# A fourth split slot in the down stage of two feed-forward layers, in place of two sum buffers

## The chip, the cores and the metric

The kernel runs on one core of one Trainium2 chip. The metric is the device time of one execution in microseconds (us), read as the median of several executions.

## The reference

The reference is one transformer block on 256 tokens of width 2048: a first feed-forward layer, a mixer, a second feed-forward layer, each with a residual and a layer norm. The change lies in the down projection of both feed-forward layers, the last product of

```python
def swiglu(x, w_gate, w_up, w_down):
    return (jax.nn.silu(x @ w_gate) * (x @ w_up)) @ w_down
```

Here `x` is [256, 2048], the two first weights are [2048, 5632] and `w_down` is [5632, 2048], all in float32.

## The kernel before

**Precision and units.** Every float32 operand is cut into a high part (rounded by ScalarE) and a low part (the rest, made by VectorE), and each product takes three matmuls: high by high, high by low, low by high. The weights are streamed. A unit is two 128-row tiles of 512 columns (`UNIT_KT` = 2, 512 KB). For one unit SyncE loads it into one of 8 raw slots (`load_unit` L386, and L847 to L857 for the down stage), ScalarE writes its high part into one of 3 split slots (`whi`, `split_hi` L436 to L444), VectorE its low part (`wlo`, `split_lo` L446 to L452), and TensorE multiplies it with two halves of 128 tokens (`token_mm` L454 to L466): 2 tiles x 2 halves x 3 = 12 matmuls of 512 columns. TensorE counts finished units in the semaphore `unit_used`; ScalarE waits for it before it writes a split slot again (L443, L1053). VectorE counts low parts in `lo_done`; TensorE waits for that before a unit, and SyncE before it loads a raw slot again.

**The down stage** of layer f runs twice over w_down, for output columns 0 to 1023 (pair 0) and 1024 to 2047 (pair 1); in a pair, c = 0 and 1 are the two chunks of 512 columns. The 5632 rows are 22 units. Most are multiplied as above ("plain"). But 2 x 3 units in pair 0 and 2 x 4 in pair 1 are taken in quads (`QUADS` L205): units a = 4+q and b = 8+q with both chunks are a 2 x 2 block product of 128 tokens by 512 columns, done with 7 products instead of 8 in Strassen's manner. Such a product ("form", P1 to P7) is 6 matmuls, half of a plain unit. P1, P2 and P3 use raw weights; P5, P7, P6 and P4 use differences of weight blocks that VectorE makes first (`add`, L1146 to L1167): P5 = (a,1)-(a,0), P7 = (b,1)-(a,1), P6 = (b,1)-P5's sum, P4 = (b,0)-P6's sum. P7's is written over the raw slot of (a,1), the three others into the three buffers of `sumB` (L261). `MADE` and `made` count them in the semaphore `formed`. The token side needs sums too, S1 to S4, made once per layer from `hT` in the first items of pair 0 (`sums` L1195, `sum_hi` L1056, `sum_lo` L1188; the same `sumB` buffers hold them on the way); P3, P5, P6 and P7 wait for them (L975).

**The order of work** is written out by hand in the class `Pair` (L49 to L103). `items` is the order in which all three engines take units and forms, `raws` the order of the loads. A pair begins with plain units (10 in pair 0, 2 in pair 1); then each quad comes as a group of 7 forms mixed with 4 plain units (3 in the last group), in the order U P1 P5 U P7 P3 U P6 P2 U P4; then come the plain units that are left (the tail, from index `tail`). Pair 0 has 53 items, pair 1 has 56. The split slot of an item is that of `ring_place` (L106): item number modulo 3, but with one step back in the middle of a phase, at item 27 of pair 0 and item 29 of pair 1, which take the slot of the item two places earlier, and not three. A raw slot is loaded again once the low part of the last item that reads it is made (`released_by` L90); SyncE issues the loads in order, so one that waits holds back all behind it. The last 6 items of pair 1 have split places of their own (`edge`) and are multiplied in half passes (`down_exit` L511).

**VectorE's order** (`down_pair` L1284): for each item the sum of a form a little ahead (for P5 before the low part of the item ahead of P1's end, for P7 and P6 behind P5 and P7, for P4 one item ahead of P6), then the low part (`form_lo` L1169 or `split_lo`), then a step of the token sums (pair 0, items 2 to 9), then in the tail a step of the fold: accumulators and the four product banks of `tp` are added into `resid` (`down_add` L1222, `fold` L1252, `down_stats` L1236). Two adds of pair 0 are done behind items 2 and 3 of pair 1 (L1307).

## Time and profile before

| what | value |
|---|---|
| median of 3 executions | 1941.09 us (1940.5 to 1942.88) |
| the profiled execution | 1941.81 us, its span 1939.8 us |
| TensorE busy | 1909.5 us, 98% of the span |
| VectorE busy | 1253.9 us, 65% |
| ScalarE busy | 894.1 us, 46% |
| granted TensorE clock, mean of the span | 0.998 |
| down stage of layer 1, layer 2 | about 494 to 703 us, about 1688 to 1928 us of the span |

Matmul records overlap: one of 512 columns shows 0.39 us, but the next starts 0.227 us after it. So a gap on TensorE is best read from the starts of two matmuls. `idle before` leaves out a part of it, because the modelled end of a matmul lies behind the next one's usual start. In the profile PE is TensorE, PEld its weight loads, DVE VectorE, ACT ScalarE, POOL GpSimd, SP SyncE.

### The profile page before, as it was taken

What the parts mean: (1) busy time and instruction counts of PE and PEld (TensorE: products, weight loads), DVE (VectorE), ACT (ScalarE), POOL (GpSimd) and SP (SyncE); (2) the same over time, 40 slices, a digit from 0 to 9 for tenths busy, and PEclk for the clock granted to TensorE, in tenths of its full rate; (3) what the DMA queues carried; (4) which work ended last, traced back from release to release, by engine and by line L of the source; (5) the groups of instructions that cost most, each with busy time, mean ns of one, the idle gap of its engine ahead of it and who ended that gap; (6) DMA issues with size and microseconds to landing.
All of it is one profiled execution on the core that took longest, in us unless ns stands there. A gap on an engine that the chain in (4) does not pass through costs nothing.

```text
span 1939.8 us, 27987 instructions
## 1 busy us (share of the span) xinstructions
PE 1909.5 (98%) x10490; PEld 1617.4 (83%) x10490; DVE 1253.9 (65%) x1411; ACT 894.1 (46%) x996; POOL 66.9 (3%) x93
## 2 busy tenths in 40 slices
PE   9999999999999999999999999999999999999997
PEld 8888888888778778999999888888888888877776
DVE  5555554555887887676766958555554555587887
ACT  5444443444454553545644544444444444455452
POOL 0000000000000001300131000000000000000000
PEclk9999999999999999999999999999999999999999
DMA  8666666667565665655442067566666666545654
GB/s 304 193 187 189 189 185 189 178 193 235 157 211 182 214 219 171 212 181 161 127 133 89 23 225 243 171 186 182 186 190 197 192 187 188 189 163 184 206 190 168
DMA packets 185365, 357.37 MB, mean 184 GB/s; under 512 B 11328, under 2 KB 23616, under 8 KB 184272
## 3 DMA queue, kind: packets, MB, share of 16 engines
q1 hardware_dynamic: 183600, 347.43, 57.4%
q0 software_dynamic: 1696, 8.99, 1.4%
q8 instruction: 47, 0.77, 0.2%
q14 instruction: 22, 0.18, 0.0%
HBM read 354.28 MB, written 2.10 MB: 184 GB/s over the span
## 4 chain that ended last, share of the span: by engine, by line
PE 91%; DVE 5%; issue 1%; DMA 1%; ACT 1%; POOL 0%; POOLq 0%; SPq 0%; DVEq 0%; ACTq 0%
PE acc L463 23%; PE acc L465 23%; PE acc L464 23%; PE acc L486 3%; PE acc L488 3%; PE acc L490 3%; PE tp L985 1%; PE tp L987 1%; PE tp L986 1%; DVE wlo L451 1%; PE tp L917 1%; PE acc L985 1%; PE acc L987 1%; PE acc L986 1%; ACT whi L444 1%
## 5 line engine op out<-in xcount | busy, mean ns | idle before, releaser
L451 DVE TENSOR_TENSOR wlo<-raw,whi 128x1024 fp32r<-128x1024 f32 (+2 forms) x579 | 692.5, 1202 | 602.8 <-ACT whi L444 600.7
L444 ACT ACTIVATE whi<-raw 128x1024 fp32r<-128x1024 f32 (+2 forms) x579 | 596.6, 1037 | 815.3 <-PE acc L465 726.9
L463 PE MATMUL acc<-whi,xT 128*128 128x512 f32 (+2 forms) x1644 | 631.0, 384 | 0.8 <-ACT zab L1612 0.4
L465 PE MATMUL acc<-whi,xT 128*128 128x512 f32 (+2 forms) x1644 | 625.7, 381 | 0.0
L464 PE MATMUL acc<-wlo,xT 128*128 128x512 f32 (+2 forms) x1644 | 625.2, 380 | 0.0
L463 PEld LDWEIGHTS acc<-whi,xT 128*128 128x128 f32 x1644 | 308.7, 188 | 64.7 <-issue 1.8
L465 PEld LDWEIGHTS acc<-whi,xT 128*128 128x128 f32 x1644 | 308.7, 188 | 59.5
L464 PEld LDWEIGHTS acc<-wlo,xT 128*128 128x128 f32 x1644 | 308.9, 188 | 55.8
L463 PE MATMUL acc<-whi,hT 128*128 128x512 f32 x432 | 170.8, 395 | 6.7 <-DVE wlo L451 6.7
L464 PE MATMUL acc<-wlo,hT 128*128 128x512 f32 x432 | 168.4, 390 | 0.0
L465 PE MATMUL acc<-whi,hT 128*128 128x512 f32 x432 | 168.4, 390 | 0.0
L486 PE MATMUL acc<-xT,whi 128*128 128x256 f32 x384 | 108.7, 283 | 0.0
L488 PE MATMUL acc<-xT,whi 128*128 128x256 f32 x384 | 108.7, 283 | 0.0
L490 PE MATMUL acc<-xT,wlo 128*128 128x256 f32 x384 | 108.7, 283 | 0.0
L463 PEld LDWEIGHTS acc<-whi,hT 128*128 128x128 f32 x432 | 81.1, 188 | 32.8 <-DVE wlo L451 16.4
L465 PEld LDWEIGHTS acc<-whi,hT 128*128 128x128 f32 x432 | 81.1, 188 | 17.4
L464 PEld LDWEIGHTS acc<-wlo,hT 128*128 128x128 f32 x432 | 81.2, 188 | 15.4
L1054 ACT ACTIVATE whi<-raw 128x1024 fp32r<-128x1024 f32 x56 | 59.4, 1061 | 39.3 <-PE acc L465 25.1
L1173 DVE TENSOR_TENSOR wlo<-raw,whi 128x1024 fp32r<-128x1024 f32 x56 | 67.4, 1221 | 11.6 <-ACT whi L1054 10.2
L490 PEld LDWEIGHTS acc<-xT,wlo 128*128 128x128 f32 x384 | 73.7, 192 | 0.0
L488 PEld LDWEIGHTS acc<-xT,whi 128*128 128x128 f32 x384 | 73.7, 192 | 0.0
L486 PEld LDWEIGHTS acc<-xT,whi 128*128 128x128 f32 x384 | 73.7, 192 | 0.0
(345 smaller groups left out, 1854.6 us busy)
## 6 DMA issues: line engine op xcount, KB each, us to landing
raw<-in_ffn_w_down_dram SPq DMA_DIRECT2D x176, 512.0 KB, 4.7
raw<-in_ffn_w_up_dram SPq DMA_DIRECT2D x175, 512.0 KB, 3.7
raw<-in_ffn_w_gate_dram SPq DMA_DIRECT2D x174, 512.0 KB, 3.8
raw<-in_w_in_dram SPq DMA_DIRECT2D x48, 512.0 KB, 3.9
raw<-in_w_out_dram SPq DMA_DIRECT2D x32, 512.0 KB, 6.4
raw<-in_w_in_dram SPq DMA_DIRECT2D x32, 260.0 KB, 2.8
raw<-in_w_in_dram SPq DMA_DIRECT2D x16, 456.0 KB, 5.2
raw<-in_w_q_idx_dram SPq DMA_DIRECT2D x8, 512.0 KB, 3.8
```

The source lines that it names most:

```text
L444: act.activation(hi[:, s, :, 0:w], raw[:, r, :, 0:w], ACT.Copy).then_inc(hi_done, 1)
L451: dve.tensor_tensor(lo[:, s, :, 0:w], raw[:, r, :, 0:w], hi[:, s, :, 0:w].bitcast(F32), ALU.subtract).then_inc(lo_done, 1)
L463: pe.matmul(o, hi, w_hi[:, s, k, 0:width], start=first and k == 0, stop=False)
L464: pe.matmul(o, hi, w_lo[:, s, k, 0:width], start=False, stop=False)
L465: ins = pe.matmul(o, lo, w_hi[:, s, k, 0:width], start=False, stop=last and k == UNIT_KT - 1)
L486: pe.matmul(o, whi[:, s, k, cols], hi, start=first and k == 0 and c == 0, stop=False, skip_group_check=True)
L488: pe.matmul(o, whi[:, s, k, cols], lo, start=False, stop=False, skip_group_check=True)
L490: ins = pe.matmul(o, wlo[:, s, k, cols], hi, start=False, stop=end, skip_group_check=True)
L985: pe.matmul(o, x_hi, w_hi[:, s, k], start=i == touches[0] and k == 0, stop=False)
L986: pe.matmul(o, x_hi, w_lo[:, s, k], start=False, stop=False)
L1054: act.activation(w_hi[:, s], form_raw(p, i), ACT.Copy).then_inc(hi_done, 1)
L1173: dve.tensor_tensor(w_lo[:, s], form_raw(p, i), w_hi[:, s].bitcast(F32), ALU.subtract)\
```

## The change

The group order becomes U P1 P3 P5 U P7 P6 U P2 P4 U, and the loads of a group U (a,0) (b,1) (a,1) U U (b,0) U. Pair 0 begins with 13 plain units, and its sums of tokens are spread over items 2 to 14. P6's sum is written over the raw slot of (a,0), P5's and P4's share one buffer `form_sum`, and the 8 KB per partition that two sum buffers took become a fourth split slot, used from item 16 of pair 0 on (before that the token sums lie there). `split_slots` hands out the split slots first in, first out, through both pairs, so an item of the groups and tails takes the slot of the item four places earlier; the step back in the middle is gone. VectorE makes each form's sum behind the low part of the item two places ahead. The raw slots of (a,0) and (b,0) are held until the low part of the item ahead of P4 (that is P2), (b,1) until that of the item ahead of P6. The fold takes P7's and P5's banks one by one: 8 counted steps in place of 7. The diff, cut:

```diff
@@ -63,13 +63,13 @@
             q = quads.index((a, b))
-            self.raws += [(a, 0), (a, 1), some[0], (b, 1), some[1], (b, 0), *some[2:]]
-            forms = [("P1", "P5"), ("P7", "P3"), ("P6", "P2"), ("P4",)]
+            self.raws += [some[0], (a, 0), (b, 1), (a, 1), *some[1:3], (b, 0), *some[3:]]
+            forms = [("P1", "P3", "P5"), ("P7", "P6"), ("P2", "P4"), ()]
...
                 self.items += [(form, q, 0) for form in forms[k]]
-        self.tail = len(self.items)
+        self.tail = 1 + max(i for i, item in enumerate(self.items) if item[0] == "P4")
@@ -85,12 +85,22 @@
         a, b = self.quads[x]
-        return self.raws.index({"P1": (a, 0), "P7": (a, 1), "P2": (b, 0), "P3": (b, 1)}[what])
+        return self.raws.index({"P1": (a, 0), "P6": (a, 0), "P7": (a, 1), "P2": (b, 0), "P3": (b, 1)}[what])
+    def item(self, form, q):
+        return self.items.index((form, q, 0))
...
-        return max(i for i, (what, _, _) in enumerate(self.items)
-                   if what not in ("P4", "P5", "P6") and self.raw_of(i) == r)
+        last = max(i for i, (what, _, _) in enumerate(self.items)
+                   if what not in ("P4", "P5") and self.raw_of(i) == r)
+        for q, (a, b) in enumerate(self.quads):
+            if self.raws[r] in ((a, 0), (b, 0)):
+                return max(last, self.item("P4", q) - 1)
+            if self.raws[r] == (b, 1):
+                return max(last, self.item("P6", q) - 1)
+        return last
@@ -101,6 +111,22 @@
+def split_slots(pairs, one_more_from, kept_apart):
...
+    free, places = list(range(SPLIT_SLOTS)), [{}, {}]
+    user = {}
+    for pair, plan in enumerate(pairs):
+        for i in range(len(plan.items) - (kept_apart if pair else 0)):
+            if (pair, i) == (0, one_more_from):
+                free.insert(0, SPLIT_SLOTS)
+            s = free.pop(0)
+            free.append(s)
+            places[pair][i] = s, user.get(s)
+            user[s] = pair, i
+    return places, user
@@ -205,8 +231,10 @@
     ENDS = [*range(4), *range(12, DOWN_U)]
-    PAIRS = [Pair(QUADS[:3], sorted(ENDS + [7, 11]), sorted(ENDS + [7, 11]), 10, (4, 4, 4)),
-             Pair(QUADS, ENDS, ENDS, 2, (4, 4, 4, 3))]
+    PAIRS = [Pair(QUADS[:3], sorted(ENDS + [7, 11]), sorted(ENDS + [7, 11]), 13, (4, 4, 4)),
+             Pair(QUADS, ENDS, ENDS, 2, (4, 4, 4, 4))]
+    FOURTH_FROM = 16
+    SPLITS, LAST_USER = split_slots(PAIRS, FOURTH_FROM, EDGES)
@@ -259,6 +287,9 @@
         sumB = mz("sumB", 88, [P, 3, UNIT_KT, BANK])
+        form_sum = mz("form_sum", 88, [P, UNIT_KT, BANK])
+        fourth_hi = mz("fourth_hi", 92, [P, 1, UNIT_KT, BANK], F32R)
+        fourth_lo = mz("fourth_lo", 96, [P, 1, UNIT_KT, BANK], F32R)
@@ -401,6 +432,17 @@
                 return edge_hi, edge_lo, slot, st.index(p, 0, edge_free(slot))
+            if plan_of(p) is not None:
+                f, pair = (0, 1)[p in DOWN[1]], (0, 1)[p in (F1DB, F2DB)]
+                s, before = SPLITS[pair][u] if u < n else (u - n, LAST_USER[u - n])
+                if before is not None:
+                    free = st.index(DOWN[f][before[0]], 0, before[1] + 1)
+                elif s < SPLIT_SLOTS:
+                    last = [v for v in range(2 * KU) if ring_place(v, 2 * KU, SPLIT_SLOTS) == s][-1]
+                    free = st.index(GU[f], GATE_CHUNKS - 1, last + 1)
+                else:
+                    free = None
+                return (whi, wlo, s, free) if s < SPLIT_SLOTS else (fourth_hi, fourth_lo, 0, free)
@@ -858,7 +900,7 @@
         SUM_ORDER = [0, 2, 1, 3]
-        FOLDS = 7
+        FOLDS = 8
@@ -869,7 +911,7 @@
-        SUM_STEPS = ["A21", "A22", "S1", "S1 low", "A11", "S3", "S2", "A12", "S4", "S3 low", "S2 low", "S4 low"]
+        SUM_STEPS = ["A21", "A22", "S1", "A11", "S1 low", "S3", "S2", "A12", "S4", "S3 low", "S2 low", "S4 low"]
@@ -896,9 +938,8 @@
-            name = plan_of(p).items[i][0]
-            if name in ("P5", "P6", "P4"):
-                return sumB[:, ("P5", "P6", "P4").index(name)]
+            if plan_of(p).items[i][0] in ("P5", "P4"):
+                return form_sum[:]
@@ -1050,7 +1091,10 @@
                     act.wait_ge(raw_loaded[v % RAW_SLOTS], st.loaded(p, 0, v))
-                act.wait_ge(unit_used, free)
+                if free is None:
+                    act.wait_ge(sem("formed"), summed(f, "S4 low"))
+                else:
+                    act.wait_ge(unit_used, free)
@@ -1069,18 +1113,19 @@
                     if p == DOWN[f][0]:
-                        if i == 4:
-                            sum_hi(0, 2)
...
                             hT_act(act, f, GATE_CHUNKS)
-                        if i == 8:
+                        if i == 7:
+                            sum_hi(0, 2)
+                        if i == 11:
                             sum_hi(1, 1)
+                        if i == 12:
                             sum_hi(2, 0)
-                        if i == 9:
+                        if i == 13:
...
@@ -1145,26 +1190,32 @@
-                first = p == DOWN[f][0] and q == 0
-                a, b = plan_of(p).quads[q]
+                pair, plan = DOWN[f].index(p), plan_of(p)
+                a, b = plan.quads[q]
+                corner = raw_ready(dve, p, a, 0)
                 if name == "P5":
-                    upper, left = raw_ready(dve, p, a, 1), raw_ready(dve, p, a, 0)
-                    if first:
-                        dve.wait_ge(sem("formed"), summed(f, "S4 low"))
-                    elif q == 0:
-                        dve.wait_ge(sem("formed"), folded(f, 0, FOLDS))
-                    dve.tensor_tensor(sumB[:, 0], upper, left, ALU.subtract).then_inc(sem("formed"), 1)
+                    upper = raw_ready(dve, p, a, 1)
+                    if q > 0:
+                        dve.wait_ge(lo_done, st.index(p, 0, plan.item("P4", q - 1) + 1))
+                        dve.wait_ge(hi_done, st.index(p, 0, plan.item("P4", q - 1) + 1))
+                    else:
+                        dve.wait_ge(sem("formed"), folded(f, 0, FOLDS) if pair else summed(f, "S4 low"))
+                    dve.tensor_tensor(form_sum[:], upper, corner, ALU.subtract).then_inc(sem("formed"), 1)
...
                     block, right = raw_ready(dve, p, b, 1), raw_ready(dve, p, a, 1)
+                    dve.wait_ge(sem("formed"), made(f, p, "P5", q))
...
                 if name == "P6":
+                    block = raw_ready(dve, p, b, 1)
+                    dve.wait_ge(lo_done, st.index(p, 0, plan.item("P1", q) + 1))
+                    dve.wait_ge(hi_done, st.index(p, 0, plan.item("P1", q) + 1))
                     dve.wait_ge(sem("formed"), made(f, p, "P5", q))
-                    dve.tensor_tensor(sumB[:, 1], raw_ready(dve, p, b, 1), sumB[:, 0], ALU.subtract)\
-                       .then_inc(sem("formed"), 1)
+                    dve.tensor_tensor(corner, block, form_sum[:], ALU.subtract).then_inc(sem("formed"), 1)
...
                     left = raw_ready(dve, p, b, 0)
+                    dve.wait_ge(lo_done, st.index(p, 0, plan.item("P5", q) + 1))
                     dve.wait_ge(sem("formed"), made(f, p, "P6", q))
-                    dve.tensor_tensor(sumB[:, 2], left, sumB[:, 1], ALU.subtract).then_inc(sem("formed"), 1)
+                    dve.tensor_tensor(form_sum[:], left, corner, ALU.subtract).then_inc(sem("formed"), 1)
@@ -1198,25 +1249,30 @@
                     sum_of(2, *block(B_KT, 1))
+                if i == 4:
...
                     sum_made(0, 2, 1, 2, ALU.add)
-                if i == 5:
-                    sum_lo(0, 2)
...
                     hT_dve(dve, f, GATE_CHUNKS)
+                if i == 7:
                     sum_of(0, *block(A_KT, 0))
-                if i == 7:
+                if i == 8:
+                    sum_lo(0, 2)
+                if i == 9:
...
                     sum_made(1, 1, 0, 1, ALU.subtract)
+                if i == 10:
                     sum_made(2, 0, 2, 0, ALU.subtract)
-                if i == 8:
+                if i == 11:
...
                     sum_of(2, *block(B_KT, 0))
+                if i == 12:
...
                     sum_lo(1, 1)
-                if i == 9:
+                if i == 13:
                     sum_lo(2, 0)
+                if i == 14:
@@ -1251,23 +1307,24 @@
-                last, u2 = sumB[:, 0, 0], sumB[:, 0, 1]
+                one, two = form_sum[:, 0], form_sum[:, 1]
...
                     dve.wait_ge(sem("sum_act"), sum_act(f, 4 + pair))
-                    fold_resid(pair, 0, 0, last)
-                    dve.tensor_tensor(u2, p_bank("P6"), last, ALU.add).then_inc(sem("formed"), 1)
+                    fold_resid(pair, 0, 0, one)
+                    dve.tensor_tensor(two, p_bank("P6"), one, ALU.add).then_inc(sem("formed"), 1)
...
                     dve.wait_ge(sem("formed"), folded(f, pair, 2))
-                    dve.tensor_tensor(sumB[:, 1], tp[:, 2:4], u2.unsqueeze(1).to_broadcast([P, 2, BANK]), ALU.add)\
-                       .then_inc(sem("formed"), 1)
+                    dve.tensor_tensor(one, p_bank("P7"), two, ALU.add).then_inc(sem("formed"), 1)
+                    dve.wait_ge(sem("formed"), folded(f, pair, 3))
+                    fold_resid(pair, 0, 1, one)
...
@@ -1286,22 +1343,15 @@
                 for i in range(LEAD if pair == 0 else 0, len(plan.items)):
-                    what, q, _ = plan.items[i]
-                    after = plan.items[i + 1] if i + 1 < len(plan.items) else ("", 0, 0)
-                    if after[0] == "P1":
-                        add(p, "P5", after[1])
-                    if what == "P5":
-                        add(p, "P7", q)
-                    if what == "P7":
-                        add(p, "P6", q)
-                    if after[0] == "P6":
-                        add(p, "P4", after[1])
-                    if what == "unit":
+                    if plan.items[i][0] == "unit":
...
                         sums(i)
+                    soon, of, _ = plan.items[min(i + 2, len(plan.items) - 1)]
+                    if soon in MADE:
+                        add(p, soon, of)
...
                     if pair == 1 and i in (2, 3):
```

## Rows read from the trace of the kernel before

**Rows 1.** The page's chain that ended last, shares of the span.

```profile
PE 91%; DVE 5%; issue 1%; DMA 1%; ACT 1%; POOL 0%; POOLq 0%; SPq 0%; DVEq 0%; ACTq 0%
```

**Rows 2.** Waits of TensorE, 494 to 722 us, then 1690 to 1940: total, times, longest.

```profile
PE acc L463 <- DVE wlo L451: 3.4, 3, 1.7
PE acc L985 <- DVE wlo L1173: 1.2, 1, 1.2
PE tp L985 <- DVE wlo L1173: 0.2, 1, 0.2
...
PE tp L985 <- DVE wlo L1173: 1.1, 1, 1.1
```

**Rows 3.** Timeline of TensorE at stalls: start, duration, instruction, idle before and releaser.

```profile
522.80 0.39 PE L465 MATMUL acc<-whi,hT 128*128 128x512 f32 x1
524.90 0.50 PE L463 MATMUL acc<-whi,hT 128*128 128x512 f32 x1 [1.71 <-DVE wlo L451]
525.24 0.39 PE L464 MATMUL acc<-wlo,hT 128*128 128x512 f32 x1
...
535.74 0.39 PE L987 MATMUL acc<-whi,sumA 128*128 128x512 f32 x1
536.07 0.50 PE L463 MATMUL acc<-whi,hT 128*128 128x512 f32 x1
...
556.54 0.39 PE L987 MATMUL acc<-whi,sumA 128*128 128x512 f32 x1
558.04 0.50 PE L463 MATMUL acc<-whi,hT 128*128 128x512 f32 x1 [1.11 <-DVE wlo L451]
...
1916.54 0.50 PE L463 MATMUL acc<-edge,hT 128*128 128x512 f32 x1 [0.82 <-DVE edge L451]
```

**Rows 4.** Timeline of ScalarE: plain units, then a form's high part, then item 27.

```profile
495.16 1.06 ACT L444 ACTIVATE whi<-raw 128x1024 fp32r<-128x1024 f32 x1 [1.72 <-PE acc L465]
497.88 1.06 ACT L444 ACTIVATE whi<-raw 128x1024 fp32r<-128x1024 f32 x1 [1.66 <-PE acc L465]
...
523.74 1.06 ACT L1054 ACTIVATE whi<-sumB 128x1024 fp32r<-128x1024 f32 x1 [2.11 <-DVE sumB L1156]
...
555.66 1.06 ACT L444 ACTIVATE whi<-raw 128x1024 fp32r<-128x1024 f32 x1 [3.13 <-PE tp L987]
```

**Rows 5.** Timeline of VectorE: end of the head, item 27, and a fold of pair 0.

```profile
519.99 2.35 DVE L1192 TENSOR_TENSOR sumA<-sumB,sumA 128x1024 fp32r<-128x1024 f32 x2
522.48 1.23 DVE L1156 TENSOR_TENSOR sumB<-raw 128x1024 f32<-128x1024 f32 x1
523.62 1.22 DVE L451 TENSOR_TENSOR wlo<-raw,whi 128x1024 fp32r<-128x1024 f32 x1
...
556.76 1.23 DVE L451 TENSOR_TENSOR wlo<-raw,whi 128x1024 fp32r<-128x1024 f32 x1 [1.14 <-ACT whi L444]
...
597.03 0.68 DVE L1258 TENSOR_TENSOR sumB<-tp,sumB 128x512 f32<-128x512 f32 x1
...
599.15 1.22 DVE L1261 TENSOR_TENSOR sumB<-tp,sumB 128x1024 f32<-128x1024 f32 x1
```

**Rows 6.** Three loads issued close together (L857): issue times, then us to landing; three windows.

```profile
L857 SPq DMA_DIRECT2D raw<-in_ffn_w_down_dram x3: 368/368/468, 1725.9 to 1727.0; - x3
...
DMA to landing us min/median/max: 3.9/4.9/5.5
...
L857 SPq DMA_DIRECT2D raw<-in_ffn_w_down_dram x3: 368/368/468, 532.6 to 533.8; - x3
...
DMA to landing us min/median/max: 4.0/5.7/7.8
...
L857 SPq DMA_DIRECT2D raw<-in_ffn_w_down_dram x3: 367/468/469, 1803.4 to 1804.3; - x3
...
DMA to landing us min/median/max: 5.1/7.4/8.8
```

**Rows 7.** Timeline of ScalarE at the start of pair 1 in layer 2.

```profile
1811.27 1.06 ACT L444 ACTIVATE whi<-raw 128x1024 fp32r<-128x1024 f32 x1 [3.71 <-DMA raw<-in_ffn_w_down_dram]
```

More of the change, by code:

```diff
@@ L1082, in ffn_act @@
                         act.wait_ge(unit_used, st.index(p, 0, plan.tail))
-                        act.activation(sumB[:, 0, 0], p_bank("P1"), ACT.Copy).then_inc(sem("sum_act"), 1)
+                        act.activation(form_sum[:, 0], p_bank("P1"), ACT.Copy).then_inc(sem("sum_act"), 1)
         def resid_add(dve, p, c, scale, in_phase, t):
@@ L1238, in down_stats @@
                 dve.wait_ge((acc0_free, acc1_free)[c][t], (n0, n1)[c][DOWN[f][pair]] + 1)
-                dve.wait_ge(sem("formed"), folded(f, pair, 5))
+                dve.wait_ge(sem("formed"), folded(f, pair, 4))
                 col = (2 * pair + c) * BANK
@@ L1252, in fold @@
             def fold(pair, step):
-                last, u2 = sumB[:, 0, 0], sumB[:, 0, 1]
+                one, two = form_sum[:, 0], form_sum[:, 1]
                 if step == 0:
                     dve.wait_ge(sem("sum_act"), sum_act(f, 4 + pair))
-                    fold_resid(pair, 0, 0, last)
-                    dve.tensor_tensor(u2, p_bank("P6"), last, ALU.add).then_inc(sem("formed"), 1)
+                    fold_resid(pair, 0, 0, one)
+                    dve.tensor_tensor(two, p_bank("P6"), one, ALU.add).then_inc(sem("formed"), 1)
                 if step == 1:
                     dve.wait_ge(sem("formed"), folded(f, pair, 2))
-                    dve.tensor_tensor(sumB[:, 1], tp[:, 2:4], u2.unsqueeze(1).to_broadcast([P, 2, BANK]), ALU.add)\
-                       .then_inc(sem("formed"), 1)
+                    dve.tensor_tensor(one, p_bank("P7"), two, ALU.add).then_inc(sem("formed"), 1)
+                    dve.wait_ge(sem("formed"), folded(f, pair, 3))
+                    fold_resid(pair, 0, 1, one)
                 if step == 2:
-                    dve.wait_ge(sem("formed"), folded(f, pair, 3))
-                    fold_resid(pair, 1, 0, sumB[:, 1, 0])
-                    fold_resid(pair, 0, 1, sumB[:, 1, 1])
+                    dve.tensor_tensor(two, p_bank("P5"), two, ALU.add).then_inc(sem("formed"), 1)
+                    dve.wait_ge(sem("formed"), folded(f, pair, 5))
+                    fold_resid(pair, 1, 0, two)
                 if step == 3:
-                    dve.tensor_tensor(last, p_bank("P5"), sumB[:, 1, 1], ALU.add).then_inc(sem("formed"), 1)
-                    dve.wait_ge(sem("formed"), folded(f, pair, 6))
-                    fold_resid(pair, 1, 1, last)
+                    dve.tensor_tensor(one, p_bank("P5"), one, ALU.add).then_inc(sem("formed"), 1)
+                    dve.wait_ge(sem("formed"), folded(f, pair, 7))
+                    fold_resid(pair, 1, 1, one)
             def pair_end(pair, i):
```

## The prediction

> **What bounds the kernel now.** The chain of waits comes first: 91% of it is TensorE [rows 1], so only what TensorE waits for can be won, and any idle time of the other engines is free. The waits of TensorE come next, and only in the two stretches of the down stage, which the change touches: 4.8 us in 5 waits in layer 1. In layer 2 the first two rows come again with the same numbers, the third is 1.1 instead of 0.2, and an edge item adds 0.8: 6.5 us in 6 waits. All are waits for a low part of VectorE [rows 2, 3]. The timeline says what a wait costs in full, read from the starts. The usual distance of two matmuls is 0.227 us. At 522.80 the next start is 2.10 later and the one after it 0.34 later: 1.87 + 0.11 lost, against 1.71 shown as idle [rows 3]. So each wait costs 0.27 more than its row. Besides, some units arrive just in time (535.74 to 536.07 is 0.10 too long, and so is the next distance), about 0.2 each, 4 or 5 times a layer, 0.9 in all. Lost and removable: layer 1 4.8 + 5 x 0.27 + 0.9 = 7.1 us, layer 2 6.5 + 6 x 0.27 + 0.9 = 9.0, together 16.1. That is the ceiling of the gain. The number of matmuls does not change.
>
> **Why it waits.** Four distances carry the rest. A plain unit takes TensorE 2.72 us (the high parts start at 495.16 and 497.88), a form half of that, 1.36; a group of 4 units and 7 forms 20.4. From the start of a high part to the start of its low part are 1.10 (555.66 to 556.76), from there to TensorE's start 1.28 (556.76 to 558.04), and VectorE starts an operation of 1024 elements every 1.14 when nothing holds it (522.48 to 523.62), 1.35 when it reads what the one before wrote (the second of the pair at 519.99 starts 1.14 later, the next at 522.48) [rows 3 to 5]. A high part starts some 0.2 after TensorE has left the item whose slot it takes. A form's own high part starts 1.26 behind the start of its sum (522.48 to 523.74) [rows 4, 5]. With three slots an item is thus ready 0.2 + 1.10 + 1.28 = 2.58 after the start of the item two before it, which leaves 0.14 where two forms lie between, and less than nothing where VectorE is busy with a sum, or at the step back in the middle, where the slot is that of the item two earlier.
>
> **The change, part by part.**
>
> 1. The end of the head. Two low parts of token sums and P5's sum stand ahead of the low part of item 10 [rows 5], and cost 1.98. They are spread now. I follow VectorE with t = 0 at TensorE's start of item 12, TensorE at 0, 2.72, 5.44 (P1), 6.80 (P3), 8.16 (P5), 9.52 (unit 17). VectorE starts: low 12 at -4.14 (slot-bound), S4, S3 low, low 13 at -0.72, S2 low, low P1 at 1.56, S4 low 2.70, P5's sum 4.05 (the 1.35), low P3 5.19 (ready 6.47, 0.3 early), low P5 6.42 (its high part waits for the sum), P7's sum 7.56, low 17 at 8.70, ready at 9.98: 0.46 late. With the restart 0.1: 0.56 stays. S1 to S4 are done by 3.9, before P3 needs them. ScalarE's work per item, at most two operations of 1.06, fits into 2.72.
>
> 2. The step back in the middle goes. In pair 0 it costs 1.37 (556.54 to 558.04, less 0.227, and 0.1) [rows 3]; item 29 of pair 1 is its twin, 1.44 with 0.83 behind it. Gain 3.6 a layer.
>
> 3. Four slots in the groups. An item may be ready 2.58 after the start of the item three before it. The tightest place is now the unit behind P1 P3 P5. With TensorE's U at 0: low P5 at 1.3 (slot free at 0.2), P7's sum 2.44, low U 4.02, ready 5.3 and wanted at 6.8. Every later item of the group is at least 1.5 early. VectorE has 15 operations a group, 15 x 1.14 = 17.1 of 20.4, the same number as before. So nothing stalls, as long as the weights are there.
>
> 4. The loads. This is the price. (a,0) is now held until P2's low part is made, and SyncE issues in order, so six of a group's eight loads go out together when P2's low part is done, and P5's sum of the next group needs (a,1), the third of them. From the landing of (a,1) to the end of P2's low part VectorE has 11 operations: 10 x 1.14 + 1.22 + 0.3 for two high parts that wait for sums + 0.1 = 13.0. A round is then 13.0 + L, L from the first issue to the third landing, against TensorE's 20.4. It binds when L is over 7.4. Three loads issued together are in the trace: twelve times within the groups, L from 6.6 (1725.9 to 1727.0 + 5.5) to 9.0 (532.6 to 533.8 + 7.8), median 7.5, mean 7.5. Once, with more queued ahead, it is 9.7 [rows 6]. Those third loads were issued 1.1 us behind the first, in the change it will be 0.8, which helps little where the transfers queue. In pair 0 the first group ends with its low P2 done at 16.84 in the count of part 1, so unit U of the next group is ready at 16.84 + L + 6.07, and wanted at 30.38: late by L - 7.46. The twelve values give 0.37 as the mean of this where positive. Twice per layer, 0.1 for a restart each: 0.94. In pair 1 the first group starts with all its weights there and low P2 done at 12.1 after its U, which leaves 1.5 us of slack before the same sum comes out late; over three rounds at the median nothing is lost.
>
> A page of the Trainium skill has this cheaper: DMA: Bandwidth & Descriptors, section on the anatomy of one DMA, gives about 2.0 us fixed and bytes / 436e3 per us. By it three loads of 524,288 bytes would take 5.6 us, an estimate, and the 0.94 a layer would be nothing; the sum below would be 1.9 us lower. No burst here was that quick, so the rows decide.
>
> 5. The start of pair 1. In layer 2 ScalarE waits 3.71 us for a load there [rows 7], VectorE's adds of pair 0 pile up behind it, and P5 comes 1.28 late (0.39 in layer 1). Now the first unit of the group is third in the loads, and the extra slot lets VectorE do the tail about one item earlier. VectorE: low of item 2 at -1.4 against TensorE's start of pair 1, its add at 0.2 (it waits for pair 0's last unit), low P1 1.4, P5's sum 2.55, add and statistics, low P3 4.9, low P5 6.7 (wanted at 10.9 - 1.28). The gain is all of it, 0.46 and 1.36. Behind the waiting add stands only low P1, whose slot is freed by the same event.
>
> 6. The fold. One operation of 1024 (1.22) becomes two of 512 (0.68) [rows 5], and one dependent pair more waits 0.2: 0.3 us of VectorE per pair, in items with 2.72 us of room. In pair 0 free: P1 of pair 1 needs the last fold only 11 us later. At the end of layer 2 VectorE must hand over six items at half distance; there a wait of 0.82 is seen [rows 3]. The fourth slot lets it be up to 2.7 earlier; I count the low part of item 53 ready about 1 us early, and the 1.08 gone. If that lead were not there, 1.08 + 0.3 would stay.
>
> **Sum.** Left per layer: 0.56 + 0.94 + 0.3 for items just in time = 1.8. Gain (7.1 - 1.8) + (9.0 - 1.8) = 12.5 us. The profiled execution (1941.81, span 1939.8) would come to 1929.3; it lies 0.7 over the median, and against the median I predict 1941.09 - 12.5 = 1928.6.
>
> **Rivals.**
>
> A. No load binds (L stays under 7.2). For it: five of the twelve bursts; the page cited above would have it so. Left per layer 0.56 + 0.2: gain 14.6, 1926.5.
>
> B. Bursts of six are slower than bursts of three or four, L about 8.5. For it: 9.7 where loads were queued ahead; against: the median 7.5. Pair 0 loses 1.04 + 1.1, pair 1 3 x 1.1 - 1.5 = 1.8, with restarts 4.4 a layer, with 0.56 + 0.3: 5.3. Gain 16.1 - 10.6 = 5.5: 1935.6.
>
> C. Slower: VectorE stands idle each round before P5's sum, waiting for the third load, and the loop of loads and sums takes the place of the slots as what bounds the groups. The point where it decides: each us of L over 7.4 costs 2 in pair 0 and up to 3 in pair 1. Loss before is 16.1, so break-even is at 8 a layer: 0.9 + 2 (L - 7.4) + 3 (L - 7.4) - 1.5 = 8, L = 9.1. At L = 10 it is 12.4 a layer, 24.8 in all: 8.7 slower, 1949.8. For it: 9.0 and 9.7 were seen; against: ten of twelve are at 8.2 or less.
>
> D. The stalls move but don't go: the head's dense stretch (S3 low to P7's sum, ten VectorE operations while TensorE does six items) starts later than I have it, because there are still three slots. Each 0.3 of delay counts in full, and all of it also delays the first burst. If it costs 2 us per layer more and the edge wait stays: gain 7, 1934.
>
> **How the numbers follow.** About 0.2% (3.9 us) is what a measurement of this kernel can tell from no change. Forecast 0.45, A 0.20, B 0.14, C 0.06, D 0.07; 0.08 for L near 9, where the two kernels come out within 0.2%. Faster by over 0.2%: 0.45 + 0.20 + 0.14 + 0.07 = 0.86; within 0.08; slower 0.06. The likeliest is 1928.6. The range reaches over A (below it only the 16.1, 1925.0) and B with some room: 1925.0 to 1936.5, which leaves out C and the cases near no change.
>
> **What would show it.** Right: TensorE's waits in the two stretches fall from 11 to about 6, all under 1 us; none at item 27 of pair 0 or 29 of pair 1, none at the edge. One of about 0.5 at the unit behind the first P5. ScalarE's waits for TensorE in the groups move to the item three before. VectorE idles before P5's sum of the second and later groups, with a load as releaser, for about 0 to 2 us; six loads of L857 stand together, the third landing 7 to 8 us after the first issue. Wrong: waits of TensorE at the same unit of every group, growing from group to group, would be B or C; waits in items 14 to 20 of pair 0 over 1 us would be D.

## The result, and the profile after

The changed kernel takes 1924.74 us (median of 4, 1923.87 to 1925.47) against 1941.88 us of the kernel before beside it (median of 4, 1940.5 to 1942.88): ratio 0.9912, 95% interval 0.9895 to 0.9929. That is 17.1 us, where 12.5 were forecast, and 0.26 us below the range. The direction and most of the steps hold; the size does not.

The page after, engines and chain:

```profile
PE 1903.5 (99%) x10490; PEld 1621.3 (84%) x10490; DVE 1256.1 (65%) x1415; ACT 893.1 (46%) x996; POOL 66.9 (3%) x93
...
PE 90%; DVE 5%; DMA 2%; issue 1%; ACT 1%; POOL 0%; POOLq 0%; DVEq 0%; ACTq 0%
```

The span fell by 16.8 us, 1939.8 to 1923.0, at the same granted clock of 0.998. The number of matmuls is the same. On the chain DMA has 2% where it had 1% [rows 1]. Three loads of down weights make most of it (start on the chain, us on it):

```profile
696.26 15.35 DMA raw<-in_ffn_w_down_dram
...
1730.71 7.32 DMA raw<-in_ffn_w_down_dram
...
1751.81 7.23 DMA raw<-in_ffn_w_down_dram
```

The last two are (a,1), the third load of two bursts of part 4 in layer 2. The first is one of the last loads of layer 1's down stage; the forecast has no term for it.

TensorE's waits after, in 494 to 722 us and then in 1680 to 1923 (total, times, longest), which answer to [rows 2]:

```profile
PE acc L505 <- DVE wlo L493: 0.4, 1, 0.4
...
PE acc L505 <- DVE wlo L493: 0.7, 2, 0.4
PE acc L505 <- DVE fourth_lo L493: 0.3, 1, 0.3
```

Of eleven waits four are left, none over 0.41. The timeline of TensorE shows two of them, at the unit behind the first P5 of layer 1 and at the unit behind the second P5 of layer 2:

```profile
537.71 0.39 PE L1028 MATMUL tp<-fourth_hi,sumA 128*128 128x512 f32 x1
538.50 0.47 PE L505 MATMUL acc<-whi,hT 128*128 128x512 f32 x1 [0.41 <-DVE wlo L493]
538.81 0.40 PE L506 MATMUL acc<-wlo,hT 128*128 128x512 f32 x1
...
1743.31 0.39 PE L1028 MATMUL tp<-whi,sumA 128*128 128x512 f32 x1
1744.02 0.51 PE L505 MATMUL acc<-fourth_hi,hT 128*128 128x512 f32 x1 [0.32 <-DVE fourth_lo L493]
```

The first unit starts 0.56 too late and its second matmul another 0.08; the other one 0.48 and 0.11. From the first matmul on hT to the start of the next stage, layer 1's down stage takes 233.4 us (494.85 to 728.23) instead of 242.8 (494.90 to 737.74); layer 2's, from its first to its last matmul, 232.5 (1679.40 to 1911.85) instead of 240.5 (1688.20 to 1928.68). The work between the two was 0.7 us longer in this execution, which makes up the 16.8. Of the 17.5 us by which the two stages are shorter, about 16.0 are waits read from the starts: 16.1 + 3.5 before (the 3.5 between 721 and 738 us, which the forecast had left out), 2.4 + 1.3 after. The other 1.5 are in distances of 0.23 to 0.25 us in the items behind a wait.

That stretch, TensorE's waits from 722 to 765 us of the kernel before:

```profile
PE tp L574 <- DVE resid L739: 1.9, 1, 1.9
PE acc L463 <- DVE edge L451: 0.8, 1, 0.8
...
```

and from 714 to 757 us of the changed one:

```profile
PE tp L616 <- DVE resid L781: 0.8, 1, 0.8
...
```

The edge item waited in layer 1 exactly as in layer 2, and behind it TensorE waited 1.9 us for the first normalised columns before their transposes. After the change the first is gone and the second is 0.8.

VectorE's timeline after: the first group of pair 0 in layer 1 (S4 low, P5's sum, the unit's low part), P5's sum and P2's low part of the next groups, then P5's sum of two groups of layer 2.

```profile
531.15 1.22 DVE L1243 TENSOR_TENSOR sumA<-sumB,sumA 128x1024 fp32r<-128x1024 f32 x1
532.50 1.23 DVE L1203 TENSOR_TENSOR form_sum<-raw 128x1024 f32<-128x1024 f32 x1
...
537.13 1.22 DVE L493 TENSOR_TENSOR wlo<-raw,whi 128x1024 fp32r<-128x1024 f32 x1
...
544.03 1.22 DVE L1224 TENSOR_TENSOR wlo<-raw,whi 128x1024 fp32r<-128x1024 f32 x1
...
552.64 1.23 DVE L1203 TENSOR_TENSOR form_sum<-raw 128x1024 f32<-128x1024 f32 x1 [0.48 <-DMA raw<-in_ffn_w_down_dram]
...
564.17 1.22 DVE L1224 TENSOR_TENSOR fourth_lo<-raw,fourth_hi 128x1024 fp32r<-128x1024 f32 x1
...
572.74 1.23 DVE L1203 TENSOR_TENSOR form_sum<-raw 128x1024 f32<-128x1024 f32 x1 [0.48 <-DMA raw<-in_ffn_w_down_dram]
...
1738.11 1.23 DVE L1203 TENSOR_TENSOR form_sum<-raw 128x1024 f32<-128x1024 f32 x1 [1.80 <-DMA raw<-in_ffn_w_down_dram]
...
1759.12 1.23 DVE L1203 TENSOR_TENSOR form_sum<-raw 128x1024 f32<-128x1024 f32 x1 [2.03 <-DMA raw<-in_ffn_w_down_dram]
```

P5's sum stands 1.35 behind S4 low, and the unit's low part 4.63 behind P5's sum (4.65 was worked out). In every later group VectorE waits for a load before P5's sum, as forecast. The round is 20.1 us in layer 1 (552.64 to 572.74), just under TensorE's 20.4, and 21.0 in pair 0 of layer 2. From P5's sum to the end of P2's low part is 12.75 (552.64 to 564.17 + 1.22); with about 0.1 from the landing to the sum it is 12.9, close to the 13.0 of part 4.

The loads, three of a burst in layer 1 and in layer 2 (the line that was L857 is L899):

```profile
L899 SPq DMA_DIRECT2D raw<-in_ffn_w_down_dram x3: 368/467/469, 545.3 to 546.2; - x3
...
DMA to landing us min/median/max: 4.5/5.4/6.4
...
L899 SPq DMA_DIRECT2D raw<-in_ffn_w_down_dram x3: 368/467/469, 1729.8 to 1730.7; - x3
...
DMA to landing us min/median/max: 4.2/6.2/7.3
```

The third lands 7.3 us after the first issue in layer 1, 8.2 in layer 2. The second burst of pair 0 gives 7.2 in layer 1 and again 8.2 in layer 2.

### The profile page after: what moved, and what is told of

Same layout as the page of the kernel before. It is cut to its first block, busy times and chain, and to the rows that moved or that the text cites. A ratio compares the mean times of both kernels' runs of the same rounds, so it can differ in the third digit from the quotient of the medians.

```text
span 1923.0 us, 28047 instructions
## 1 busy us (share of the span) xinstructions
PE 1903.5 (99%) x10490; PEld 1621.3 (84%) x10490; DVE 1256.1 (65%) x1415; ACT 893.1 (46%) x996; POOL 66.9 (3%) x93
## 4 chain that ended last, share of the span: by engine, by line
PE 90%; DVE 5%; DMA 2%; issue 1%; ACT 1%; POOL 0%; POOLq 0%; DVEq 0%; ACTq 0%
PE acc L505 24%; PE acc L507 24%; PE acc L506 24%; PE acc L528 3%; PE acc L532 3%; PE acc L530 3%; DMA raw<-in_ffn_w_down_dram 2%; PE tp L1026 1%; PE tp L1028 1%; PE tp L1027 1%; PE tp L958 1%; DVE wlo L493 1%; PE acc L1026 1%; PE acc L1028 1%; PE acc L1027 1%
## 5 line engine op out<-in xcount | busy, mean ns | idle before, releaser
L493 DVE TENSOR_TENSOR wlo<-raw,whi 128x1024 fp32r<-128x1024 f32 (+2 forms) x559 | 668.0, 1201 | 576.4 <-ACT whi L486 574.8
L486 ACT ACTIVATE whi<-raw 128x1024 fp32r<-128x1024 f32 (+2 forms) x559 | 575.1, 1036 | 746.2 <-PE acc L507 676.7
L505 PE MATMUL acc<-whi,hT 128*128 128x512 f32 x352 | 137.6, 391 | 1.1 <-DVE wlo L493 1.1
L507 PE MATMUL acc<-whi,hT 128*128 128x512 f32 x352 | 137.2, 390 | 0.0
L506 PE MATMUL acc<-wlo,hT 128*128 128x512 f32 x352 | 137.2, 390 | 0.0
L505 PEld LDWEIGHTS acc<-whi,hT 128*128 128x128 f32 x352 | 66.1, 188 | 15.7 <-issue 1.6
L507 PEld LDWEIGHTS acc<-whi,hT 128*128 128x128 f32 x352 | 66.1, 188 | 13.8
L506 PEld LDWEIGHTS acc<-wlo,hT 128*128 128x128 f32 x352 | 66.1, 188 | 13.6
```

The source lines that it names most:

```text
L486: act.activation(hi[:, s, :, 0:w], raw[:, r, :, 0:w], ACT.Copy).then_inc(hi_done, 1)
L493: dve.tensor_tensor(lo[:, s, :, 0:w], raw[:, r, :, 0:w], hi[:, s, :, 0:w].bitcast(F32), ALU.subtract).then_inc(lo_done, 1)
L505: pe.matmul(o, hi, w_hi[:, s, k, 0:width], start=first and k == 0, stop=False)
L506: pe.matmul(o, hi, w_lo[:, s, k, 0:width], start=False, stop=False)
L507: ins = pe.matmul(o, lo, w_hi[:, s, k, 0:width], start=False, stop=last and k == UNIT_KT - 1)
```

## The experiments

Ten kernels ran. Three take the gain apart, one prices the loop of loads, four follow what was left (the changed kernel itself as their base), two price the order of the work.

**Without the fourth slot.** The order of items, loads and sums stays.

```diff
-    FOURTH_FROM = 16
+    FOURTH_FROM = 999
```

> The changed kernel with its order of items, loads and sums, but the fourth slot never handed out. Theory (the fourth slot is what removes the stalls, the order alone does not): TensorE waits about 0.8 to 1.0 us at the unit behind P1 P3 P5 in each of the 7 groups of a layer, and the waits at the edge of both layers (1.1 each) and before the first transposes in layer 1 come back: 12 to 17 us over the changed kernel, 1937 to 1942 us. Rival (the order of items and the first-in-first-out places do the work, the slot is idle reserve): under 4 us over the changed kernel, 1925 to 1929 us.

1942.85 us against 1942.15 beside it, ratio 1.0005 (0.9995 to 1.0015): the whole gain is gone. Its waits of TensorE in layer 1, 494 to 760 us:

```profile
PE acc L505 <- DVE wlo L493: 3.9, 7, 0.6
PE tp L616 <- DVE resid L781: 1.8, 1, 1.8
PE acc L505 <- DVE edge L493: 1.1, 1, 1.1
...
```

Seven waits, one in each group, at the unit behind P1 P3 P5; the edge wait and the long one before the transposes are back. Layer 2 has the same seven, and in three groups a wait of 0.2 to 0.5 before P3 as well. A wait costs 0.7 to 0.9 with its restart, a little under the 0.8 to 1.0 expected, and the time lies 0.85 over the bound that was written. The rival falls.

**The kernel before, three slots first in, first out.** `split_slots` and its places are put into the kernel before, with no fourth slot and nothing else changed.

```diff
+    SPLITS, LAST_USER = split_slots(PAIRS, 999, EDGES)
...
+            if plan_of(p) is not None:
...
+                return whi, wlo, s, free
```

(The branch is for the down stage; the other stages keep `ring_place`.)

> The kernel before, with its three split slots handed out first in, first out; nothing else changed. Theory (the two steps back in the middle of a pair cost 1.37 and 1.44 with 0.83 behind it, in each layer): 5.6 to 7.3 us under the kernel before, 1934.5 to 1936.5 us; the waits at item 27 of pair 0 and item 29 of pair 1 are gone and the other waits stay. Rival (those items are late because VectorE is behind, and the places do not matter): within 1.5 us of the kernel before.

1935.44 us, ratio 0.9965 (0.9953 to 0.9978), 6.7 us faster. The waits of TensorE from 540 to 700 us are a single one, at the start of pair 1 (the one of 1.7 in the head of each layer stays, as do the start of pair 1 in layer 2 and the edge):

```profile
PE tp L1011 <- DVE wlo L1199: 0.3, 1, 0.3
```

So places alone, with neither a slot nor another order, win 6.7 us in the kernel before. And with three slots the new arrangement (order, loads, one shared buffer, sums two ahead) is worse than the old one by 1942.85 - 1935.44 = 7.4 us, with its waits behind the three forms in a row.

**No fourth slot in the tail of pair 1.** It is handed out until item 44 and then taken away.

```diff
                 free.insert(0, SPLIT_SLOTS)
+            if (pair, i) == (1, plan.tail):
+                free.remove(SPLIT_SLOTS)
```

> The changed kernel, but the fourth slot is taken away again from the tail of pair 1 on (from item 45). Theory (VectorE's lead of one more item at the exit ended the edge wait in both layers and about 1 us of TensorE's wait before the first transposes of layer 1): both edge waits of about 0.8 us idle are back and the wait before the transposes goes from 0.8 to about 1.9; 3 to 3.5 us over the changed kernel, 1928 us. Rival (the edge was late by the loads, which now stand earlier in a burst, or by the old fold): no edge wait, within 0.7 us of the changed kernel.

1929.32 us, 4.6 over the changed kernel. Waits of TensorE in layer 1:

```profile
PE tp L618 <- DVE resid L783: 1.9, 1, 1.9
PE acc L507 <- DVE edge L495: 1.1, 1, 1.1
...
```

Both are back. From the starts each edge wait costs 1.41 (two layers; part 6 had set 1.08 + 0.3 for the case without the lead), the wait before the transposes 1.09 more: 3.9, and the two waits in the groups of layer 2 are 0.2 longer in this execution; the rest is not settled. The exit's gain is the lead of one more item, in both layers, and not the order of the loads or the fold. It is a quarter of the whole.

**(a,1) as the sixth load of the burst.**

```diff
-            self.raws += [some[0], (a, 0), (b, 1), (a, 1), *some[1:3], (b, 0), *some[3:]]
+            self.raws += [some[0], (a, 0), (b, 1), *some[1:3], (b, 0), (a, 1), *some[3:]]
```

> The changed kernel with (a,1) as the sixth load of a burst instead of the third. Theory (a round of VectorE is 13.0 us plus the landing of (a,1), against 20.4 of TensorE): landing about 9.9 to 10.4 us after the burst's first issue, a round of 23 to 23.4, VectorE idle before P5's sum in every later group, and 10 to 13 us of waits of TensorE more per layer: 1945 to 1951 us, slower than the kernel before. Rival (VectorE has slack enough in the new order, and loads do not bind): under 6 us over the changed kernel, under 1931 us.

1971.21 us, ratio 1.0151 (1.0135 to 1.0168), 46.5 over the changed kernel and 20 over the upper bound. The direction and the mechanism hold, the landing was set too low. In layer 1 the first sixth load is issued 3.0 us behind the first and lands 11.4 after it (548.1 + 8.4 - 545.1), not 9.9 to 10.4, and the round of VectorE is 24.0. The six loads, and P5's sum of two groups of layer 1:

```profile
L899 SPq DMA_DIRECT2D raw<-in_ffn_w_down_dram x6: 368/468/979, 545.1 to 548.1; - x6
...
DMA to landing us min/median/max: 4.4/6.9/8.4
```

```profile
556.58 1.23 DVE L1203 TENSOR_TENSOR form_sum<-raw 128x1024 f32<-128x1024 f32 x1 [4.74 <-DMA raw<-in_ffn_w_down_dram]
...
580.59 1.23 DVE L1203 TENSOR_TENSOR form_sum<-raw 128x1024 f32<-128x1024 f32 x1 [4.47 <-DMA raw<-in_ffn_w_down_dram]
```

24.0 - 20.4 = 3.6 are lost in this group, and TensorE's waits there are 2.99 before P3 and 0.59 at the unit behind P5. In layer 2 the same two sums stand 25.3 apart, behind longer waits for the load:

```profile
1763.17 1.23 DVE L1203 TENSOR_TENSOR form_sum<-raw 128x1024 f32<-128x1024 f32 x1 [6.45 <-DMA raw<-in_ffn_w_down_dram]
...
1788.47 1.23 DVE L1203 TENSOR_TENSOR form_sum<-raw 128x1024 f32<-128x1024 f32 x1 [6.26 <-DMA raw<-in_ffn_w_down_dram]
```

The sixth load lands 11.1 to 11.4 us after the first issue in four of the five bursts of layer 1, 12.8 in the fifth, and 12.2 to 13.3 in layer 2. In all ten later groups P5's sum starts 0.1 behind that landing, and the next burst 12.8 to 12.9 behind the sum, 13.4 once. So the rule of part 4, a round of 13.0 + L, holds to 0.2 but for that one. From the first P5's sum of a pair to its last one, the four pairs together take 42.6 us more than in the changed kernel, nearly all of the 46.5.

TensorE's clock fell too. Stretches of 25 us in layer 2 of this kernel (TensorE busy, weight loads, VectorE, ScalarE, POOL, granted clock, DMA share, GB/s):

```profile
1790.00:1815.00 25.00, 24.02 (x94) 19.65 (x95) 21.72 (x21) 13.87 (x14) 0.00 (x0) 0.86 0.41 139
1815.00:1840.00 25.00, 25.00 (x112) 20.71 (x111) 20.14 (x24) 9.66 (x10) 0.00 (x0) 1.00 0.65 221
```

In the first, TensorE is idle for only 1.0 us, but gets through 94 matmuls where the second has 112: part of it ran at the lower of the two clock levels, 1.2 instead of 2.4 GHz, after idle times of 4.3 us before 1765.7 and 3.0 before 1791.0. From 1791.5 to 1796.7 its matmuls start 0.43 apart and not 0.23. Over the kernel some 50 matmuls do so, about 10 us in all, but most of them take the place of a wait, since the loads and VectorE set the round. What is left for the clock, in the last group of a pair, and for everything else is 46.5 - 42.6 = 3.9.

**The changed kernel again, and three ways to take what is left.** They ran beside it.

> The changed kernel once more, as the base for the three kernels beside it. All theories: 1923 to 1926 us.

1924.67 us (1924.53 to 1925.48). The first edit puts (b,1) and (a,1) ahead of (a,0), so that they don't wait behind it:

```diff
-            self.raws += [some[0], (a, 0), (b, 1), (a, 1), *some[1:3], (b, 0), *some[3:]]
+            self.raws += [some[0], (b, 1), (a, 1), (a, 0), *some[1:3], (b, 0), *some[3:]]
```

> The changed kernel with the loads of a group as U (b,1) (a,1) (a,0) U U (b,0) U, so that (b,1) and (a,1) are issued once the low part of P7 is made, ahead of the burst, and (a,0) is the burst's first. Theory (the waits of TensorE in the second and third group of pair 0 in layer 2, 0.59 and 0.54, come from the landing of (a,1) late in the burst): both gone, VectorE's waits for a load before P5's sum under 0.3 us in all, 1.0 to 1.2 us under the changed kernel. Rival (they come from something else in layer 2, such as VectorE's own work): they stay, same time within 0.3 us.

1922.96 us (1922.89 to 1923.08), 1.7 under the changed kernel, where 1.0 to 1.2 were expected. P5's sum of the second group of pair 0 in each layer:

```profile
552.12 1.22 DVE L1203 TENSOR_TENSOR form_sum<-raw 128x1024 f32<-128x1024 f32 x1
...
1755.16 1.22 DVE L1203 TENSOR_TENSOR form_sum<-raw 128x1024 f32<-128x1024 f32 x1
```

No P5's sum waits for a load any more, and the two waits of TensorE in the groups of layer 2 (0.61 and 0.64 with restarts in the base beside it) are gone; the wait before the transposes of layer 1 is 0.2 shorter, and the last 0.3 is open. The second edit moves the token sums of the head one item earlier:

```diff
                 if i == 6:
                     hT_dve(dve, f, GATE_CHUNKS)
-                if i == 7:
                     sum_of(0, *block(A_KT, 0))
...
-                if i == 14:
+                if i == 13:
                     sum_lo(3, 2)
```

> The changed kernel with the token sums of the head moved one item earlier (A11 behind hT's low part in item 6, S1 low in item 7, and so on, S4 low in item 13). Theory (the wait of 0.64 at the unit behind the first P5 comes from S4 low and its 0.21 of dependence ahead of P5's sum): both such waits gone, 1.2 to 1.3 us under the changed kernel; the first burst of loads starts up to 1.1 us earlier as well. Rival (the wait is set by the slots or by ScalarE's order): it stays above 0.3 us in each layer.

1922.38 us (1922.33 to 1923.12), 2.3 under the changed kernel, where 1.2 to 1.3 were expected. The wait at the unit behind the first P5 is gone in both layers (2 x 0.64), and so is, since the first burst starts earlier, one of the two in the groups of layer 2 (0.6); the wait before the transposes of layer 1 was 0.4 instead of 0.8 in this execution. Both edits together:

> Both edits together. Theory: no wait of TensorE of more than 0.1 us is left between the hidden transposes and the exit in either layer, 2.2 to 2.6 us under the changed kernel, 1922.3 us; faster than both kernels of the study. Rival: the gains do not add, because each moves the other's limit: under 1.5 us.

1921.94 us (1921.53 to 1922.53), 2.7 under the changed kernel. Between the hidden transposes of item 3 and the exit TensorE waits nowhere in either layer, and from 1680 us on its list of waits is empty. The gains do not add (1.7 + 2.3), because each takes away the wait in the second group of layer 2 (0.6), and the wait before the transposes of layer 1 is 0.8 again in this execution.

**Sums one item ahead instead of two.** Raw slots are held one item longer to match.

```diff
-                    soon, of, _ = plan.items[min(i + 2, len(plan.items) - 1)]
+                    soon, of, _ = plan.items[min(i + 1, len(plan.items) - 1)]
...
-                return max(last, self.item("P4", q) - 1)
+                return max(last, self.item("P4", q))
...
-                return max(last, self.item("P6", q) - 1)
+                return max(last, self.item("P6", q))
```

> The changed kernel, but VectorE makes each form's sum behind the low part of the item one place ahead instead of two, and the raw slots are held one item longer to match. Theory (two places ahead keeps VectorE busy with the item between while ScalarE makes the form's high part): each of the 4 sums of a group is followed by its own low part 2.36 us later instead of 1.14, and the round from P5's sum to the release of the loads grows from 13.0 to about 17.6, with the landing of (a,1) to 24 to 25 us against 20.4: 3.6 to 4.7 us of TensorE's wait in each of the 5 later groups of a layer, 1960 to 1972 us. Rival (four slots give enough lead, and where the sums stand does not matter): within 4 us of the changed kernel.

1997.19 us, ratio 1.0285 (1.0268 to 1.0303), slower than everything else here and 25 us over my upper bound. Its VectorE, layer 1: P5's sum and its low part, and P5's sum of the next group.

```profile
558.94 1.22 DVE L1203 TENSOR_TENSOR form_sum<-raw 128x1024 f32<-128x1024 f32 x1
561.28 1.23 DVE L1224 TENSOR_TENSOR wlo<-form_sum,whi 128x1024 fp32r<-128x1024 f32 x1 [1.13 <-ACT whi L1098]
...
584.42 1.22 DVE L1203 TENSOR_TENSOR form_sum<-raw 128x1024 f32<-128x1024 f32 x1
```

The 2.34 between a sum and its low part is as expected. The round is 25.5, a little over the 24 to 25 expected. What was missing in the expectation are the waits in the first group of each pair (2.0 behind 543.05, 0.4 and 0.8 before it; 1.5 in pair 1), which have nothing to do with loads, and those in the tails and at the exits. Read from the starts, 10 later groups x 5.1, 2 x 3.2 and 2 x 1.5 are 60 of the 72.5 us, and the tails and exits add 7.8. The granted clock was 0.93 in 565 to 590 us and in 665 to 690; how much of the last 4 or 5 it takes was not separated.

**The groups in the old order, with four slots** and with both edits above. The last group of each pair has 3 units; in the kernel before only pair 1 has that (its pair 0 has three groups of 4). The diff, cut:

```diff
-            self.raws += [some[0], (a, 0), (b, 1), (a, 1), *some[1:3], (b, 0), *some[3:]]
-            forms = [("P1", "P3", "P5"), ("P7", "P6"), ("P2", "P4"), ()]
+            self.raws += [some[0], (a, 1), (b, 1), (a, 0), some[1], (b, 0), *some[2:]]
+            forms = [("P1", "P5"), ("P7", "P3"), ("P6", "P2"), ("P4",)]
...
-    PAIRS = [Pair(QUADS[:3], sorted(ENDS + [7, 11]), sorted(ENDS + [7, 11]), 13, (4, 4, 4)),
-             Pair(QUADS, ENDS, ENDS, 2, (4, 4, 4, 4))]
+    PAIRS = [Pair(QUADS[:3], sorted(ENDS + [7, 11]), sorted(ENDS + [7, 11]), 13, (4, 4, 3)),
+             Pair(QUADS, ENDS, ENDS, 2, (4, 4, 4, 3))]
```

> Four slots, one shared sum buffer, sums two items ahead, head sums one item earlier and (a,1) and (b,1) loaded early, as in the kernel with both edits; but the groups in the order of the kernel before, U P1 P5 U P7 P3 U P6 P2 U P4, and the last group of each pair with 3 units. Theory (with four slots the order of the items hardly matters, it was chosen to fit the waits): no waits of TensorE over 0.5 us in the groups, 1921.5 to 1924.5 us. Rival (the new order carries a good part of the gain): waits in every group, over 1926 us.

1921.41 us (1921.16 to 1921.6), ratio 0.9893 (0.9876 to 0.9909): the fastest of all, 3.3 under the changed kernel and not to be told from the one with both edits and the new order. All its waits of TensorE from 494 to 757 us:

```profile
PE tp L616 <- DVE resid L781: 0.5, 1, 0.5
PE acc L505 <- issue: 0.2, 1, 0.2
```

From 1680 us on there are none. With four slots and the loads and sums early, it does not matter which of these two orders the products have. With three slots the old arrangement was 7.4 us the better one.

## Why the prediction was wrong in size

**The bound and the ceiling.** That TensorE bounds and that only its waits in the down stage could be won was right. The step that failed is the first one, the ceiling of 16.1: "only in the two stretches of the down stage" was read as 494 to 722 us in layer 1. The stage of layer 1 ends at 738 (not at about 703, as the table ahead of the prediction has it), so the edge wait of layer 1 (1.08) and the wait before the transposes (2.03, 0.97 after the change) were not in the sum. The ceiling of 16.1 was too low by 3.5, and the sum by 1.08 + 1.06 = 2.1. The range ended at that ceiling, and the result lies beyond it. The sign was in the rows: an edge wait in one layer and none in the other, where both layers run the same code.

**1, the head.** Right: 0.46 + 0.1 was forecast, 0.56 + 0.08 measured in both layers; the experiment with the sums one item earlier takes it away.

**2, the step back.** Right: 3.6 a layer, 7.2 in all, was forecast; the kernel before with its places alone changed gains 6.7.

**3, four slots.** Right: behind the head no wait stays in a group in which the loads are there in time. Without the slot the same order, loads and sums are no faster than the kernel before, so they win only together with it.

**4, the loads.** The mechanism was right in every part: six loads together, VectorE waiting before P5's sum with a load as releaser, a round of 13.0 + L. The size was too high: 0.94 was set down for each layer, measured 0 in layer 1 and 0.48 + 0.11 + 0.43 + 0.11 = 1.1 in layer 2, 0.8 less in all. L was 7.3 and 8.2 in the two bursts shown, inside the 6.6 to 9.0. Only what lies over 7.46 costs anything in pair 0: layer 1's two bursts there (7.3, 7.2) lay under it and layer 2's (8.2, 8.2) over it. The 8.2 should then have cost 0.74 and cost 0.48. Why loads land later in layer 2 no run shows. The Trainium skill (DMA: Bandwidth & Descriptors, the anatomy of one DMA) has the rule that the prediction cites for DMAs issued through GpSimd, and the loads here are issued by SyncE. Worked out for three loads it gives 5.6 us, an estimate; no burst of the changed kernel was that quick (7.1 at the least), so the trace does not agree, and its 0 for this term is further from the 1.1 than the 1.9 that were set down.

**5, the start of pair 1.** Right: no wait is left there in either layer, 0.46 and 1.36 gone.

**6, the fold and the edge.** Right where it looked, in layer 2, and shown by the tail without the slot, where the edge wait is 1.41. The same gain in layer 1 is the miss above.

**The sum.** 2.3 for the exit of layer 1 (with its just-in-time starts), 0.8 for the loads, 0.6 for items just in time of which none is left, 1.5 in the slightly longer distances behind a wait, too small for my reading of starts; less 0.2 for the head and 0.7 for the work between the layers. Together 4.3, the difference between 12.5 and the 16.8 us of the spans. The last 0.3, from 16.8 to 17.1, is within the scatter of the runs.

**The rivals.** A comes nearest (one of the layers behaved as it says), B and C did not happen. C is real all the same: with (a,1) late the kernel is slower than before by 29 us. Its slope is right as well: put the ten landings of that run in its formula, and it gives 46.1 of waits less the 16.1, 30.0 us slower. D did not happen.

## What to carry to other kernels

Before summing what a change can win, find where its stage ends from its last instruction, and check that each wait in one copy of a repeated stage has its twin in the other. Where stalls are many and small, count the distance between items that share a buffer first: a buffer plan that hands slots out first in, first out was worth 6.7 us here for nothing, and with one more slot the two orders of work that were tried came out the same. When buffers are released late by design, look at which loads of the next round queue behind the late one; moving two free loads ahead of it was worth 1.7 us.

## What the runs showed of the hardware

With (a,1) late, TensorE's granted clock was 0.86 over a 25 us stretch in which the engine was idle for only 1.0 us, behind waits of 4.3 and 3.0; with the sums one item ahead it was 0.93 in 565 to 590 us, behind waits of 1.8 before 562.7 and 1.9 before 570.8. In the kernel before, with single waits of up to 1.9, it was 1.00 in every full stretch of 25 us of both down stages. An operation of 1024 elements on VectorE is followed by the next after 1.14 us, but after 1.35 when that one waits for it to be done (531.15 to 532.50). Six loads of 512 KB issued within 3 us landed 4.4 to 11.4 us after the first issue, 1.3 to 1.6 us apart; in layer 2 the sixth landed up to 13.3 after it.
